# Root-mean-square normalisations of the mixers: logarithms read from PSUM, own buffers and a new order in the first mixer

## The reference, cut to what matters

```python
def ab_mixer(h, positions, w_in, gate_up, gate_b, out_norm, q_norm, k_norm, w_out):
    (gq, gk, gv, glow, gr, dq, dk, dv, iq, ik, iw) = split_cols(h @ w_in, AB_SPLITS)
    ...
    o_gla = rms_norm(o_gla, out_norm) * jax.nn.silu(gr)        # gated linear attention, 4 heads of 128
    q = rope(rms_norm(dq, q_norm), positions)                  # 4 heads of 128
    k = rope(rms_norm(dk, k_norm), positions)
    ...
    o_dsa = dsa_attention(q, k, v, iq, ik, iw, n_sel)          # keys chosen by the indexer's scores
    return jnp.concatenate([o_gla, o_dsa], axis=-1) @ w_out
```

## Time and profile before

| | |
|---|---|
| three runs | 1888.47, 1893.04, 1898.57 us; median 1893.04 |
| the profiled execution | 1893.83 us, its span 1892.5 us |
| busy share of the span | PE 88%, PEld 53%, DVE 34%, ACT 19%, POOL 2% |
| mean granted TensorE clock | 0.94 of 2.4 GHz |
| DMA | 577.31 MB, mean 305 GB/s |
| chain that ended last | PE 69%, DMA 21%, DVE 7%, ACT 2%, issue 1% |

### The profile page before, as it was taken

How to read it: one execution, slowest core, us unless ns; L and a number is a source line. 1 busy time by engine, 2 the same in 40 slices (tenths; PEclk the granted TensorE clock), 3 DMA queues, 4 the chain that set the end, 5 groups by cost and what they waited for, 6 DMA issues and landing times.

```text
span 1892.5 us, 20547 instructions
## 1 busy us (share of the span) xinstructions
PE 1671.0 (88%) x8735; PEld 1002.8 (53%) x8735; DVE 652.6 (34%) x1264; ACT 363.9 (19%) x632; POOL 32.4 (2%) x39
## 2 busy tenths in 40 slices
PE   3998799999979999999799988989879787897877
PEld 2775699997669999757533322333223222232223
DVE  6566278754757554344400100101001010010102
ACT  2212244342334443132101000000000000000001
POOL 0101000000000000100010000000000000000000
PEclk7989989999999999999889988999889999898999
DMA  9554348744646555123569999999999999999996
GB/s 397 231 217 178 109 163 329 267 178 184 254 168 244 202 179 223 60 87 120 222 242 417 427 431 431 423 401 427 430 430 429 430 429 429 431 431 430 427 431 264
DMA packets 43548, 577.31 MB, mean 305 GB/s; under 512 B 4785, under 2 KB 5954, under 8 KB 7234
## 3 DMA queue, kind: packets, MB, share of 16 engines
q1 hardware_dynamic: 43458, 576.00, 74.4%
HBM read 574.93 MB, written 1.05 MB: 304 GB/s over the span
## 4 chain that ended last, share of the span: by engine, by line
PE 69%; DMA 21%; DVE 7%; ACT 2%; issue 1%; SPq 0%; DVEq 0%; ACTq 0%
DMA RING_T<-in_w_up 20%; PE P L997 18%; PE P L420 13%; PE P L1022 6%; PE P L707 4%; PE P L708 4%; PE P L709 4%; PE P L429 3%; PE P L728 2%; PE P L727 2%; PE P L726 2%; PE P L975 2%; DVE RING_T L1569 2%; PE P L1039 2%; DMA RING_T<-in_ada_w 1%
## 5 line engine op out<-in xcount | busy, mean ns | idle before, releaser
L997 PE MATMUL P<-RING_T,SCR 128*34 128x512 f32 x1008 | 483.6, 637 | 116.1 <-DMA RING_T<-in_w_up 116.1
L998 PE MATMUL P<-RING_T,SCR 128*34 128x512 f32 x992 | 477.5, 638 | 0.0
L997 PEld LDWEIGHTS P<-RING_T,SCR 128*34 128x34 f32 x1008 | 114.5, 119 | 432.8 <-issue 432.3
L2118 DVE TENSOR_TENSOR SCR<-P,SCR 34x512 f32<-34x512 f32 x64 | 44.4, 693 | 595.4 <-ACT SCR L1477 595.4
L1022 PE MATMUL P<-RING_T,SCR 128*34 128x512 f32 x512 | 227.3, 594 | 9.0 <-DMA RING_T<-in_w_down 9.0
L1023 PE MATMUL P<-RING_T,SCR 128*34 128x512 f32 x512 | 227.3, 594 | 0.0
L707 PE MATMUL P<-SCF 128*128 128x256 f32 x704 | 205.8, 292 | 16.0 <-DVE SCF L1849 10.9
L708 PE MATMUL P<-SCF 128*128 128x256 f32 x704 | 203.1, 289 | 0.0
L420 PE MATMUL P<-HWC,RING_T 128*128 128x256 f32 (+1 forms) x832 | 196.1, 394 | 7.9 <-ACT HWC L1121 4.1
L709 PE MATMUL P<-SCF 128*128 128x256 f32 x704 | 203.0, 288 | 0.0
L420 PEld LDWEIGHTS P<-HWC,RING_T 128*128 128x128 f32 x832 | 161.1, 195 | 40.4 <-issue 14.1
(11 more groups left out here) (252 smaller groups left out, 1728.6 us busy)
## 6 DMA issues: line engine op xcount, KB each, us to landing
RING_T<-in_w_gate SPq DMA_DIRECT2D x63, 2048.0 KB, 16.6
RING_T<-in_w_down SPq DMA_DIRECT2D x63, 2048.0 KB, 13.3
RING_T<-in_w_up SPq DMA_DIRECT2D x62, 2048.0 KB, 12.3
RING_T<-in_ada_w SPq DMA_DIRECT2D x24, 2048.0 KB, 10.1
RING_T<-in_ffn_w SPq DMA_DIRECT2D x22, 2048.0 KB, 8.2
RING_T<-in_ffn_w SPq DMA_DIRECT2D x22, 1024.0 KB, 4.9
RING_T<-in_ab_w_in SPq DMA_DIRECT2D x7, 2048.0 KB, 17.3
RING_T<-in_w_in SPq DMA_DIRECT2D x6, 2048.0 KB, 8.1
```

Source lines behind the costliest of these rows:

```text
L997: pe.matmul(u.t[0:CAP, :], xs, wg.v(KC, 512)[:, c, :], start=c == 0, stop=c == KC - 1)
L998: ins = pe.matmul(u.t[64:64 + CAP, :], xs, wu.v(KC, 512)[:, c, :], start=c == 0, stop=c == KC - 1)
```

## The change

1. In every normalisation ScalarE takes the logarithm straight from the PSUM bank, with scale 1/n and eps as bias. VectorE reads the bank for v only once that logarithm is done, and its next step that needs v waits for it by semaphore.
2. In the first mixer the cosine products go to `cos_tmp`: for the queries in the tile `V`, for the keys in the tile `AT`, both free once gla_o is done (two waits on POOL and two on ACT see to that). Row 0 of `bufs` then holds squares alone.
3. VectorE's order is: pairs dq, go, dk, rotation of the queries, `select(0, 18)`, rotation of the keys. ScalarE makes the squares of go as soon as the sums of dq have been read by TensorE, and those of the keys as soon as those of go have been.
4. TensorE runs dk's first chunk between the two halves of gla_o, the sums of squares of the keys ahead of the rotation of the queries, and waits for the two halves of the keys one by one.
5. The silu gate comes behind the last eviction of av. The out-projection's first four chunks are split: the products with rows 4 to 7 of `MIX` for all four banks, then the wait for mix, then those with rows 0 to 3.

The same products, sums and functions are computed; the logarithm's argument is scaled on ScalarE instead of VectorE.

```diff
@@ line 339 of the kernel before @@
         assert s.at <= 21440, s.at
+
+    def cos_tmp(self, qk, z):
+        a = self.AT.rearrange("p a b c -> p (a b c)") if qk else self.V.rearrange("p a b -> p (a b)")
+        return a[:, 512 * z:512 * z + 512].rearrange("p (a b) -> p a b", b=T)
@@ line 609 of the kernel before @@
         ins.then_inc(bb[par].full, 1)
+        if par == 0:
+            chunk("dk", 0)
     score(0, 0)
-    chunk("dk", 0)
     score(0, 1)
@@ line 622 of the kernel before @@
     pe_rows(nc, k, ("dv", 0), w.v(KC, 512), k.HX, 0, 128)
+    pe_norm(nc, k, "dk0", v.bufs[0][:, 0, :], "nsq", 5)
+    pe_norm(nc, k, "dk1", v.bufs[1][:, 0, :], "nsq", 6)
     pe.wait_ge(s["norm"], 2)
...
     w.left = (u.full, u.n)
-    pe_norm(nc, k, "dk0", v.bufs[0][:, 0, :], "nsq", 5)
-    pe_norm(nc, k, "dk1", v.bufs[1][:, 0, :], "nsq", 6)
     chunk("gr", 0)
     chunk("gr", 1)
-    pe.wait_ge(s["norm"], 6)
-    pe_rope(nc, k, "rope_k0", "rot128", v.KA[:, 0:2, :])
-    pe_rope(nc, k, "rope_k1", "rot128", v.KA[:, 2:4, :])
+    for z in range(2):
+        pe.wait_ge(s["norm"], 5 + z)
+        pe_rope(nc, k, f"rope_k{z}", "rot128", v.KA[:, 2 * z:2 * z + 2, :])
     chunk("gr", 2)
@@ line 665 of the kernel before @@
-    pe.wait_ge(s["mix"], 1)
     for i in range(2):
         pe.wait_ge(P["av", i].taken, P["av", i].done)
-    pe_out_proj(nc, k, "ab", [("abo", 0), ("abo", 1)], v.MIX, T)
+
+    w = ring["abo", 0]
+    pe.wait_ge(w.sem, w.n)
+    bb = [pe_bank(nc, k, ("ab", "out", j)) for j in range(4)]
+    for j in range(4):
+        for c in range(4, KC):
+            pe.matmul(bb[j].t[:, 0:T], w.v(KC, 512)[:, c, j * 128:(j + 1) * 128], v.MIX[:, c, :], start=c == 4, stop=False)
+    pe.wait_ge(s["mix"], 1)
+    for j in range(4):
+        for c in range(4):
+            ins = pe.matmul(bb[j].t[:, 0:T], w.v(KC, 512)[:, c, j * 128:(j + 1) * 128], v.MIX[:, c, :], start=False, stop=c == 3)
+        ins.then_inc(bb[j].full, 1)
+    w.left = (bb[3].full, bb[3].n)
+    w = ring["abo", 1]
+    pe.wait_ge(w.sem, w.n)
+    for j in range(4):
+        u = pe_chunk(nc, k, ("ab", "out", 4 + j), w.v(KC, 512), j, v.MIX, T)
+    w.left = (u.full, u.n)
     pe_out_stat(nc, k, "ffn0", M)
@@ line 1088 of the kernel before @@
-def act_rms(nc, k, name, v, a):
+def act_rms(nc, k, name, ps, n, a):
...
     i, s, u = RMS_AT[name], k.sem, k.banks["rms", name]
-    nc.scalar.wait_ge(u.taken, u.done)
-    nc.scalar.activation(a, v, ACT.Ln).then_inc(s["ln"], 1)
+    nc.scalar.wait_ge(u.full, u.n)
+    nc.scalar.activation(a, ps, ACT.Ln, bias=k.cc("eps"), scale=1.0 / n).then_inc(s["ln"], 1)
     nc.scalar.wait_ge(s["ln"], 2 * i + 1)
...
 def act_stat(nc, k, name, c0):
-    act_rms(nc, k, name, k.RS[:, 1, 0:L - c0], k.RS[:, 2, 0:L - c0])
+    act_rms(nc, k, name, k.banks["rms", name].t[:, 0:L - c0], D, k.RS[:, 2, 0:L - c0])
...
 def act_head(nc, k, name, m):
-    act_rms(nc, k, name, m[:, 2, :], m[:, 3, :])
+    act_rms(nc, k, name, k.banks["rms", name].t[:, :], 128, m[:, 3, :])
@@ line 1211 of the kernel before @@
     act_head(nc, k, "dq1", v.bufs[1])
-    chunk("dk", 1, v.KA[:, 1, :])
-    act.wait_ge(s["norm"], 1)
-    square(0, flat(v.OT)[:, 0:512])
-    act.wait_ge(s["norm"], 2)
-    square(1, flat(v.OT)[:, 512:1024])
-    chunk("dk", 2, v.KA[:, 2, :])
-    chunk("dk", 3, v.KA[:, 3, :])
-    act_head(nc, k, "go0", v.bufs[0])
-    act_head(nc, k, "go1", v.bufs[1])
+
+    for z in range(2):
+        act.wait_ge(P["gla_o", z].taken, P["gla_o", z].done)
+    for z in range(2):
+        u = P["rms", f"dq{z}"]
+        act.wait_ge(u.full, u.n)
+        square(z, flat(v.OT)[:, 512 * z:512 * z + 512])
+    for j in range(1, 4):
+        chunk("dk", j, v.KA[:, j, :])
+    act.wait_ge(P["dk", 3].taken, P["dk", 3].done)
+    act.wait_ge(P["dk", 0].taken, P["dk", 0].done)
+    for z in range(2):
+        act.wait_ge(s["norm"], 1 + z)
+        act_head(nc, k, f"go{z}", v.bufs[z])
+        square(z, flat(v.KA)[:, 512 * z:512 * z + 512])
     act_out(nc, P["dv", 0], v.VA[:, 0, :], P["dv", 0].t[:, :])
-    act.wait_ge(s["rope"], 4)
-    square(0, flat(v.KA)[:, 0:512])
-    act.wait_ge(s["rope"], 5)
-    square(1, flat(v.KA)[:, 512:1024])
+    for z in range(2):
+        act.wait_ge(s["norm"], 3 + z)
+        act_head(nc, k, f"dk{z}", v.bufs[z])
     act_out(nc, P["dv", 1], v.VA[:, 1, :], P["dv", 1].t[:, :])
-    act_head(nc, k, "dk0", v.bufs[0])
-    act_head(nc, k, "dk1", v.bufs[1])
     act.wait_ge(s["score"], 17)
@@ line 1242 of the kernel before @@
             act_out(nc, P["pt", i, j], v.PT[:, o:o + 4, :], P["pt", i, j].v(4, 128))
-        if i:
-            act.wait_ge(P["gr", 3].taken, P["gr", 3].done)
-            act_table(nc, SET_SILU)
-            act.activation(flat(v.RL), flat(v.RL), ACT.Silu).then_inc(s["silu_g"], 1)
-            act_table(nc, SET_EXP)
         act_out(nc, P["av", i], v.MIX[:, 4:8, i * 128:(i + 1) * 128], P["av", i].v(4, 128))
+    act.wait_ge(P["gr", 3].taken, P["gr", 3].done)
+    act_table(nc, SET_SILU)
+    act.activation(flat(v.RL), flat(v.RL), ACT.Silu).then_inc(s["silu_g"], 1)
+    act_table(nc, SET_EXP)
     for c in range(KC):
@@ line 1410 of the kernel before @@
     def subln(hd):
-        act_rms(nc, k, f"sl{hd}", v.bufs[hd % 2][:, 2, 0:L], v.bufs[hd % 2][:, 3, 0:L])
+        act_rms(nc, k, f"sl{hd}", P["rms", f"sl{hd}"].t[:, 0:L], 128, v.bufs[hd % 2][:, 3, 0:L])
@@ line 1517 of the kernel before @@
-def dve_rms(nc, k, name, ps, n, r, v, a):
+def dve_rms_begin(nc, k, name, ps, n, r, v, a):
...
     i, s, u = RMS_AT[name], k.sem, k.banks["rms", name]
-    nc.vector.wait_ge(u.full, u.n)
+    nc.vector.wait_ge(s["ln"], 2 * i + 1)
     nc.vector.tensor_scalar(v, ps, 1.0 / n, EPS, ALU.mult, ALU.add).then_inc(u.taken, 1)
...
     nc.vector.tensor_tensor(r, a, a, ALU.mult).then_inc(s["rs"], 1)
+
+
+def dve_rms_end(nc, k, name, r, v, a):
+
+    i, s, u = RMS_AT[name], k.sem, k.banks["rms", name]
+    nc.vector.wait_ge(u.taken, u.done)
     nc.vector.wait_ge(s["rs"], 3 * i + 1)
...
+def dve_rms(nc, k, name, ps, n, r, v, a):
+    dve_rms_begin(nc, k, name, ps, n, r, v, a)
+    dve_rms_end(nc, k, name, r, v, a)
+
+
 def rms_done(name):
@@ line 1539 of the kernel before @@
-def dve_head(nc, k, name, m, src, weight, count):
-
-    dve_rms(nc, k, name, k.banks["rms", name].t[:, :], 128, m[:, 1, :], m[:, 2, :], m[:, 3, :])
-    nc.vector.wait_ge(k.sem["rs"], rms_done(name))
-    nc.vector.scalar_tensor_tensor(out=src, in0=src, scalar=weight, in1=m[:, 1, :], op0=ALU.mult, op1=ALU.mult).then_inc(k.sem["norm"], 1)
+def dve_heads(nc, k, name, bufs, src, weight):
+    def begin(z):
+        m, n = bufs[z], f"{name}{z}"
+        dve_rms_begin(nc, k, n, k.banks["rms", n].t[:, :], 128, m[:, 1, :], m[:, 2, :], m[:, 3, :])
+
+    def end(z):
+        m, n, x = bufs[z], f"{name}{z}", src[:, 512 * z:512 * z + 512]
+        dve_rms_end(nc, k, n, m[:, 1, :], m[:, 2, :], m[:, 3, :])
+        nc.vector.wait_ge(k.sem["rs"], rms_done(n))
+        nc.vector.scalar_tensor_tensor(out=x, in0=x, scalar=weight, in1=m[:, 1, :], op0=ALU.mult, op1=ALU.mult).then_inc(k.sem["norm"], 1)
+
+    begin(0)
+    end(0)
+    begin(1)
+    end(1)
@@ line 1769 of the kernel before @@
     QAf, KAf, OTf = flat(v.QA), flat(v.KA), flat(v.OT)
-    dve_head(nc, k, "dq0", v.bufs[0], QAf[:, 0:512], k.vv("dsa_q"), 1)
-    dve_head(nc, k, "dq1", v.bufs[1], QAf[:, 512:1024], k.vv("dsa_q"), 2)
-    dve_head(nc, k, "go0", v.bufs[0], OTf[:, 0:512], k.vv("gla_out"), 3)
-    dve_head(nc, k, "go1", v.bufs[1], OTf[:, 512:1024], k.vv("gla_out"), 4)
+    dve_heads(nc, k, "dq", v.bufs, QAf, k.vv("dsa_q"))
+    dve_heads(nc, k, "go", v.bufs, OTf, k.vv("gla_out"))
+    dve_heads(nc, k, "dk", v.bufs, KAf, k.vv("dsa_k"))
+    dve_rope(nc, k, "rope_q0", v.QA[:, 0:2, :], v.cos_tmp(0, 0), s128, 4, "rope", "cosm")
+    dve_rope(nc, k, "rope_q1", v.QA[:, 2:4, :], v.cos_tmp(0, 1), s128, 5, "rope", "cosm")
     dve.wait_ge(s["score"], at[0])
     select(0, 18)
-    dve_rope(nc, k, "rope_q0", v.QA[:, 0:2, :], tmp(0), s128, 4, "rope", "cosm")
-    dve_rope(nc, k, "rope_q1", v.QA[:, 2:4, :], tmp(1), s128, 5, "rope", "cosm")
-    dve_head(nc, k, "dk0", v.bufs[0], KAf[:, 0:512], k.vv("dsa_k"), 5)
-    dve_head(nc, k, "dk1", v.bufs[1], KAf[:, 512:1024], k.vv("dsa_k"), 6)
-    dve_rope(nc, k, "rope_k0", v.KA[:, 0:2, :], tmp(0), s128, 6, "rope", "cosm")
-    dve_rope(nc, k, "rope_k1", v.KA[:, 2:4, :], tmp(1), s128, 7, "rope", "cosm")
+    dve_rope(nc, k, "rope_k0", v.KA[:, 0:2, :], v.cos_tmp(1, 0), s128, 6, "rope", "cosm")
+    dve_rope(nc, k, "rope_k1", v.KA[:, 2:4, :], v.cos_tmp(1, 1), s128, 7, "rope", "cosm")
     for n, i in enumerate((1, 0)):
@@ line 1895 of the kernel before @@
     dve_ada(nc, k, 1, 4, 5)
-    dve_head(nc, k, "sq0", v.bufs[0], Qf[:, 0:512], k.vv("sb_q"), 7)
-    dve_head(nc, k, "sq1", v.bufs[1], Qf[:, 512:1024], k.vv("sb_q"), 8)
-    dve_head(nc, k, "sk0", v.bufs[0], Kf[:, 0:512], k.vv("sb_k"), 9)
-    dve_head(nc, k, "sk1", v.bufs[1], Kf[:, 512:1024], k.vv("sb_k"), 10)
```

(18 more changed lines are left out.)

## The result

| | before | after | forecast |
|---|---|---|---|
| median of 4 runs, us | 1890.76 | 1867.92 (1866.33 to 1872.96) | 1875.6 (1867 to 1886) |
| ratio, 95% interval | | 0.988 (0.9854 to 0.9905) | |
| profiled execution, us | 1893.83 | 1872.96 | 1875.6 |

What follows compares the result with a forecast made beforehand. VectorE, with waits in it, was taken as the chain in the rewritten stretch before the experts' DMA stream. Terms -0.9, -10.7, -2.2, -2.4 and -2.0 sum to -18.2 us on 1893.83, giving 1875.6 us, range 1867 to 1886.

Steps and rivals of the forecast that it cites:

- Heads, -10.7: First mixer's normalisations and rotations: TensorE ends last and the logits begin at 172.6 us instead of 183.27.
- Rival 1: First mixer: VectorE ends last, held by GpSimd's four cosine products 2.4 to 5.1 us, losing 0 to 2.7; chance 0.15.
- One of the prediction's signs of being wrong: Before the logits: VectorE instructions of 1.2 us beside GpSimd, with TensorE waiting at the logits.
- mix0, -0.9: Layer norm mix0: VectorE comes late, ScalarE will have finished, so the whole 0.93 us wait goes.
- the clock's gain on gla_o: TensorE at half clock in 120 to 125 us; up to 1.0 us more won if that shortens.
- Gate, -2.2: Between softmax and out-projection: the out-projection starts at +7.15 us instead of +9.37 us.
- the 2.0 of the clock: Out-projection: its 8 chunks take 29.92 us instead of 28; up to 2.0 us more won at better clock.
- in the sum both stay: Both TensorE clock losses, at 120 to 125 us and in the out-projection, were taken as unchanged in the sum.
- Layer norms, -0.4 each: ffn0, mix1, ffn1, mix2, ffn2 and fin: chain falls from 1.41 to 1.0 us, six times 0.4, -2.4 in all.
- sk, -2.0: Second mixer: pair sk on VectorE's chain to the stick-breaking goes from 2 x 4.88 to 0.75 + 7.04 us.
- rival 2: Gain ends in the DMA stream or an unseen wait: 1886 us without the heads' term, 1893 without any; chance 0.10.
- Rival 3: TensorE at 1.2 GHz between 141 and 172 us: 31 us more, time 1906 us; chance 0.03.

Runs made afterwards that it cites:

- experiments 3 and 4: First: kernel before with only the new gate and split out-projection, ratio 0.9986. Second: changed kernel with the old gate and out-projection, ratio 0.9908.

## Why the prediction was right, and which terms were not

- **Heads, -10.7: right (-10.35), with a wrong chain behind it.** The forecast had 31.3 us of TensorE from dk's end to the logits; they were 31.1 (137.31 to 168.43, where gr 2 ends) plus the wait of 1.20. **Who ends last was wrong**: I had TensorE last with VectorE 1.8 us behind; VectorE was last. The step that failed is the dense chain of 3.52 us a call with GpSimd at no cost. Rival 1 had the mechanism and its size right (2.4 to 5.1 us; measured 2.8), and I gave it 0.15: the earlier trace rows spoke for it, and I held against it that some products would meet instructions with one input. Each of the four lengthened an instruction with two.

  By the rival's own sum, 2.4 us of VectorE are free, so 0.4 us are lost, and that is what the distance shows: 35.46 us where the forecast has 35.1. So the number came out right because the two chains are nearly equally long, and not because GpSimd costs nothing. The wait on TensorE is longer than 0.4 because its dk chunks had ended 3.30 us behind the first head step, where the forecast took 3.9 from the profile of before. One of the prediction's signs of being wrong stands in the profile: VectorE instructions of over 1.2 us beside GpSimd, with TensorE waiting at the logits.

  The Trainium skill, "SBUF — State Buffer", section "Who interferes with whom", says that a VectorE instruction with two SBUF inputs contends with a GpSimd instruction that reads SBUF, and that one with at most one SBUF input does not, outside of certain modes. The trace agrees on both sides: with two SBUF inputs 0.68 us became 1.27 to 1.47, and the selection's instructions with one input kept their 0.28 and 0.29.
- **mix0, -0.9: right (-0.89), but 2.4 us more came in behind it.** The first head step hangs on a load of modulation weights that VectorE waits for (idle 5.92 us before, 5.54 after, released by the DMA), and SP issues it when TensorE has left a slot: at 111.98 before, at 109.16 after. TensorE was ahead because its clock was 1.00 in 39 to 42 us instead of 0.50 (the two windows, before and then after). Most of this is chance, as the same window of all 14 profiles tells. At half clock there the first head step came at 135.6 to 136.4 us with the new logarithm (3 profiles) and at 137.5 and 137.6 with the old; at full clock at 134.0 to 134.6 (7 profiles) and at 135.4 and 135.8. So the clock in that window is worth 1.9 us with either logarithm, and at the same clock the new logarithm is ahead by 1.4 us: mix0's 0.9 and 0.5 more whose cause no run shows. I had looked at the squares of dq, not at this load, and put the clock's gain on gla_o at up to 1.0.

```profile
39.00:42.00 3.00, 2.55 (x6) 1.11 (x7) 2.85 (x6) 1.88 (x4) 0.00 (x0) 0.50 1.01 431
```
```profile
39.00:42.00 3.00, 3.00 (x14) 1.68 (x13) 2.83 (x6) 1.79 (x5) 0.00 (x0) 1.00 0.99 423
```

  The load itself, first reader on VectorE before and after:

```profile
120.27 1.23 DVE L1569 SCALAR_TENSOR_TENSOR RING_T<-RING_T,CB 128x1024 f32<-128x1024 f32 x1 [5.92 <-DMA RING_T<-in_ada_w]
```
```profile
117.27 1.22 DVE L1618 SCALAR_TENSOR_TENSOR RING_T<-RING_T,CB 128x1024 f32<-128x1024 f32 x1 [5.54 <-DMA RING_T<-in_ada_w]
```

- **Gate, -2.2: right (-2.21), and the 2.0 of the clock that I left out of the sum came in too.** Of the 2.2, 0.8 is the last av at full clock. The step "in the sum both stay" failed: experiments 3 and 4 tie this term to the gate's part. With it the sum would have been 1873.6.
- **Layer norms, -0.4 each: right.** From TensorE's sum of squares to VectorE's first product of the layer it was 4.01 us before and 3.60 after at ffn1. The distances in the table cannot show 0.4: of the 1.46 us to mix1's step, 1.4 belong to the one execution of before (208.43; 207.03 in its second profile). The logarithm took 0.47 us over 256 columns and 0.69 over 512, where I had 0.52 and 0.70. **sk, -2.0: right**: mix1's step to the stick-breaking's first product 49.15 and 47.26.
- **The stream carried it** (rival 2 fell): at ffn2's step the changed kernel is 23.5 us ahead; 2.45 of it are lost in the experts' stream, whose length was 958 to 967 us over all profiles, before and after. At ffn0's step it is 18.4 us ahead, of which the sum names 14.2 (0.9 + 10.7 + 2.2 + 0.4); the rest is nearly all clock, 1.9 ahead of the first head step and 2.0 in the out-projection.
- **Rival 3 fell**: from 137 to 172 us TensorE ran at full clock throughout.

The forecast of 1875.6 was 2.6 us above the profiled execution and 7.7 above the median. Of the 7.7, 3.1 are the base (the profiled execution of before stood at 1893.83 where its median came out at 1890.76), and 4.6 the gain, 22.8 us where I had 18.2.

## What to carry to other kernels

When a wait for another engine is taken out of a chain, look at what had hidden in that wait: here GpSimd's products, which had cost nothing, became 2.8 us on VectorE, and they cost nothing again beside instructions with one input. A forecast that comes out right in its number can still have the wrong engine last: ask the profile for the wait, not only for the distance. A wait taken away ahead of dense TensorE work can be worth more than its own length (here 1.45 us of wait and, in three of four profiles, 2.9 of clock); look at the duration of the first products behind the wait. Take one part out at a time and read distances between landmarks: the parts here gave 5.2 and 3.6 us alone and 10.35 together, a difference that the medians of these runs are too coarse to tell.

## What the runs showed of the hardware that was not expected

- TensorE's clock behind a wait of 2.20 us was at half in 3 of 4 profiles, and never where that wait was 0.79 (10 profiles). In one of these ten it fell earlier, in av of i = 1. Behind a wait of 2.64 us before the logits it fell too (one profile), and behind waits of 1.18 to 1.34 us at that place it did not (five).
- Each VectorE instruction of 0.68 us with two SBUF inputs that started beside a cosine product of GpSimd ended 0.54 to 0.56 us behind that product (25 cases in the 14 profiles), and GpSimd's product kept its 1.26 to 1.28 us.
- Four cosine products back to back take 4.95 us on GpSimd, 1.24 each, beside VectorE's selection; a single one takes 1.27.
- Between the first two instructions of the Newton step, which depend on each other, one more semaphore wait, for a value that VectorE's own earlier instruction had set, went with a distance of 0.80 us instead of 0.72.
